# Moving weight sums of the mixing stage from VectorE to GpSimd in a fused transformer kernel

## The reference

```python
p = h @ w_in[l]                                   # q, k, v, gu, gv, conv input, gates
gl = a[..., :CONV_WIDTH] * jax.nn.sigmoid(a[..., CONV_WIDTH:])      # gated linear unit
y = depthwise_conv(gl, conv_w, taps=31) + conv_b
c_out = jax.nn.silu(layer_norm(y, norm_g, norm_b)) @ w_conv_o
gates = jax.nn.sigmoid(p[..., GATE_OFF:])                           # ga, gg, gc
return (ga * a_out + gg * g_out + gc * c_out) @ w_out
```

## Time and profile before

| | |
|---|---|
| median of three runs | 3959.73 us |
| the profiled execution, its span | 3959.4 us |
| TensorE busy | 3818.9 us, 96% |
| VectorE busy | 2353.0 us, 59% |
| ScalarE busy | 945.4 us, 24% |
| GpSimd busy | 290.0 us, 7% |
| mixing of block 0 | 555 to 1067 us |
| mixing of block 1 | 2205 to 2547 us |

### The profile page before, as it was taken

How to read it: one execution, slowest core, us unless ns; L and a number is a source line. 1 busy time by engine, 2 the same in 40 slices (tenths; PEclk the granted TensorE clock), 3 DMA queues, 4 the chain that set the end, 5 groups by cost and what they waited for, 6 DMA issues and landing times.

```text
span 3959.4 us, 34044 instructions
## 1 busy us (share of the span) xinstructions
PE 3818.9 (96%) x13274; PEld 2247.6 (57%) x13274; DVE 2353.0 (59%) x3855; ACT 945.4 (24%) x1917; POOL 290.0 (7%) x257
## 2 busy tenths in 40 slices
PE   7999899999999999999999999999999999889999
PEld 3454455555554555554445876647665458657665
DVE  5793548887405556556315699525667456835666
ACT  2102521111403111113125211321111334431111
POOL 1111000113021000000000012210000000000000
PEclk8999999999999999999999999999999999999999
DMA  7652001111212111111210112222222213011221
GB/s 262 216 198 90 6 22 58 48 55 52 96 61 59 64 64 53 54 64 54 72 68 6 64 65 85 85 101 80 85 90 88 75 34 88 9 43 64 91 96 69
DMA packets 126640, 300.51 MB, mean 76 GB/s; under 512 B 5394, under 2 KB 13634, under 8 KB 126480
## 3 DMA queue, kind: packets, MB, share of 16 engines
q1 hardware_dynamic: 108720, 239.73, 17.1%
q0 software_dynamic: 17760, 58.61, 4.5%
HBM read 296.14 MB, written 2.18 MB: 75 GB/s over the span
## 4 chain that ended last, share of the span: by engine, by line
PE 87%; DVE 8%; ACT 2%; DMA 1%; issue 1%; DVEq 0%; SPq 0%; ACTq 0%
PE psum L447 33%; PE psum L2495 15%; PE psum L2365 14%; PE psum L2419 12%; PE psum L2359 3%; PE psum L1127 2%; PE psum L2464 2%; PE psum L2447 1%; DVE sb_kvt L2813 1%; DVE sb_rc L2813 1%; PE psum L1233 1%; DMA sb_ra<-in_ada_w 1%; ACT sb_rb L2047 1%; DMA sb_ring<-in_ada_w 1%; PE psum L1253 1%
## 5 line engine op out<-in xcount | busy, mean ns | idle before, releaser
L447 PE MATMUL psum<-sb_ring,sb_rc 128*128 128x512 f32 x868 | 392.7, 594 | 7.5 <-DVE sb_rc L593 7.5
L2047 ACT ACTIVATE sb_rc<-psum 128x512 f32<-128x512 f32 (+3 forms) x295 | 147.1, 519 | 993.1 <-DVE sb_ra L609 294.7
L2903 DVE SCALAR_TENSOR_TENSOR sb_rc<-sb_rc,sb_vec 128x512 f32<-128x512 f32 (+1 forms) x450 | 384.2, 916 | 0.0
L2419 PE MATMUL psum<-sb_ring,sb_ht 128*128 128x512 f32 x832 | 364.5, 597 | 3.5 <-ACT sb_ht L2047 2.8
L447 PE MATMUL psum<-sb_ht,sb_ring 128*128 128x256 f32 (+1 forms) x1152 | 307.3, 417 | 0.0
L447 PEld LDWEIGHTS psum<-sb_ring,sb_rc 128*128 128x128 f32 x868 | 164.7, 190 | 216.6 <-issue 204.3
L2047 ACT ACTIVATE sb_rc<-sb_rc 128x512 f32<-128x512 f32 (+3 forms) x248 | 152.8, 680 | 526.2 <-DVE sb_rc L578 526.2
L2495 PE MATMUL psum<-sb_ht,sb_ring 128*128 128x384 f32 (+1 forms) x960 | 274.0, 433 | 4.0 <-DVE sb_rc L3137 4.0
L2365 PE MATMUL psum<-sb_rc,sb_ring 128*128 128x512 f32 (+1 forms) x768 | 276.6, 521 | 0.0
L2419 PEld LDWEIGHTS psum<-sb_ring,sb_ht 128*128 128x128 f32 x832 | 156.8, 191 | 205.7 <-issue 202.3
L447 PE MATMUL psum<-sb_rb,sb_rc 128*128 128x512 f32 x588 | 269.2, 594 | 0.0
(11 more groups left out here) (414 smaller groups left out, 5580.1 us busy)
## 6 DMA issues: line engine op xcount, KB each, us to landing
sb_ring<-in_w_in SPq DMA_DIRECT2D x37, 2048.0 KB, 7.9
sb_ring<-in_w_ff SPq DMA_DIRECT2D x32, 2048.0 KB, 8.0
sb_ring<-in_w_ffn SPq DMA_DIRECT2D x16, 2048.0 KB, 7.9
sb_rc<-in_ada_w POOLq DMA_DIRECT2D x26, 1024.0 KB, 5.8
sb_ra<-in_ada_w POOLq DMA_DIRECT2D x14, 1024.0 KB, 5.8
sb_ring<-in_w_gmlp_o SPq DMA_DIRECT2D x4, 2048.0 KB, 7.8
sb_ring<-in_w_attn_o SPq DMA_DIRECT2D x4, 2048.0 KB, 7.7
sb_ring<-in_w_conv_o SPq DMA_DIRECT2D x4, 2048.0 KB, 7.8
```

Source lines behind the costliest of these rows:

```text
L447: last = pe.matmul(bank(to, width), left[k], right[k], start=k == 0, stop=k == depth - 1)
L2047: return act.activation(out_, in_, f, **kw)
L2419: last = pe.matmul(bank(4 + g % 4, width), lhs[:, k, at:at + P], ring[:, slot, k, 0:width], start=k == 0, stop=k == KT - 1)
L2903: step = stt(out_, in_, vec[:, j, k:k + 1], out_, op0=ALU.mult, op1=ALU.add)
```

## The change

GpSimd gets a function `weight_sums` of its own, with the same four operations, and makes the sets of units 2 to 19 in both blocks. VectorE keeps those of units 0 and 1. For unit 2 GpSimd also waits until VectorE's two sets are counted, so that `s_mix_s` goes up in order. Sets 2 to 9 come one after another behind the pads. Sets 10 to 19 stand between the merges of branch outputs: in branches 0 and 1 one set before each of the merges 0, 2, 4 and 6, in branch 2 sets 18 and 19 before merge 0. In VectorE's order the calls are struck out and nothing is put in their place.

```diff
+            def weight_sums(l, u):
+
+                slot, loaded = mix_loaded(l, u)
+                pool.wait_ge(*loaded)
+                pool.wait_ge(*s_mix_ps.at(l, 6 * u - 7))
+                if u == 2:
+                    pool.wait_ge(*s_mix_s.at(l, 2))
+                a11, a12, a21, a22 = mix_weights(slot, u)
+                s_ = mix_sums(u)
+                tt = pool.tensor_tensor
+                ch.link(tt(s_[:, 0, :, :], a21, a22, ALU.add))
+                ch.note(tt(a21, a11, a21, ALU.subtract))
+                ch.link(tt(s_[:, 1, :, :], s_[:, 0, :, :], a11, ALU.subtract))
+                tt(s_[:, 2, :, :], a12, s_[:, 1, :, :], ALU.subtract).then_inc(s_mix_s.sem, 1)
...
+                for u in range(2, 10):
+                    weight_sums(l, u)
                 for b in range(3):
                     run = 3 * l + b
                     for j in range(KT):
+                        first = 10 + 4 * b + 2 * (j // 4)
+                        if b < 2 and j % 2 == 0:
+                            weight_sums(l, first + j % 4 // 2)
+                        if b == 2 and j == 0:
+                            weight_sums(l, 18)
+                            weight_sums(l, 19)
                         pool.wait_ge(*s_bo_sb.at(run, j + 1))
...
                     third_sum(l, u)
-                    if u < 8:
-                        weight_sums(l, u + 2)
                     if u >= 4 and (u < 9 or u % 2 == 0):
...
-                        weight_sums(l, u + 1)
                         convolve(f3)
-                        weight_sums(l, u + 2)
                         convolve(f3)
...
                     step(l, 16)
-                weight_sums(l, 18)
...
                 third_sum(l, 17)
-                weight_sums(l, 19)
```

## The result

Eight runs of the kernel with the change have the median 3969.3 us (3967.21 to 3972.81); eight of the kernel before beside them 3959.56 us (3956.65 to 3962.33). The ratio is 1.0024, with a 95% interval of 1.0014 to 1.0034: slower, by 9.7 us at the medians.

The account below looks back on a forecast made before the run. The prediction took TensorE's unbroken matmul chain as the bound, so freeing VectorE gains nothing; stalls of 3.6 + 1.8 + 1.4 + 2.9 = 9.7 us on 3959.4 gave 3969 us, range 3959 to 3986.

Parts of the forecast that it names:

- Nothing to win, and the chain: Both mixing stretches: an unbroken run of matmuls, VectorE holds nobody up, at most 1.4 us of idle TensorE to win.
- 1.02 us for each operation: VectorE's taps: delay per GpSimd operation beside them; a moved set costs a busy VectorE 4.08 us where it saved 2.66.
- Units 4 to 9: Both blocks: sets delay VectorE's third sums, TensorE waits for ScalarE's copies; 3.6 us in block 1, 1.8 in block 0.
- together 8.0: Unit 7's third sum, block 1: sets 6, 7 and 8 leave 3.9 us of lateness, set 9 adds 4.08.
- reserves of 4.4 and 6.1 us: Unit 7: slack between ScalarE's copy and the product needing it, 4.36 us in block 1, 6.1 in block 0.
- Unit 14 of block 1: Set 14 waits for the tap stream's end, merges 0 and 1 queue behind it; stall 1.4 us, ends 0 and 4.
- Before the norm: Before the convolution's norm, block 1: GpSimd's queue of sets 16, 17 and merges runs late; stall 2.9 us, ends 0 and 6.
- ScalarE waits for merge 7 before its first squares: Before block 1's norm: merge 7 ends at 2512.8, ScalarE's fourth copy of unit 16 at 2514.3, against a reserve of 1.1.
- sets 18 and 19 cost nothing: Before their units: ready 6 to 10 us ahead on a free GpSimd, no cost; 2 us if it were late.
- The base: Whole kernel: profiled span 3959.4 us, median of three runs 3959.73, with nothing but 0.3 around the span.
- The rival that the contention would be absorbed: Taps are filler, VectorE terms halve, GpSimd queue terms vanish: 2.7 us, 3962.1; chance 0.43.
- GpSimd would be the bound: At 1.8 us an operation, unit 7 and sets 10, 12, 14 run late: 32 us, 3991; chance 0.07 above 3986.

Follow-up runs that it names:

- e12: Kernel after with only sets 2 to 5 and 10 to 15 on GpSimd, VectorE waiting for its own last operation twice per long tap stream; 3960.7 us, ratio 1.0.
- e7: Kernel after, GpSimd's sets 6 to 9 waiting for the third sum of the unit two before them; 3965.6 us, single execution.
- e5a: Kernel after, first operation of sets 2 to 9 made twice on GpSimd, one more operation that reads SBUF; 3976.6 us, single execution.
- e1: Kernel after with only sets 2 to 9 of each block on GpSimd, 10 to 19 back on VectorE; 3967.1 us, ratio 1.002.
- e8: Kernel after, one convolution tap less in three places of each of units 4 to 8, five more behind units 10, 12 and 14; 3969.0 us, single execution.
- e9: Kernel after, VectorE waiting for its own last operation at two places of the long tap streams behind units 9, 11, 13 and 15; 3971.0 us, single execution.
- e6: Kernel after, set 17 put behind merge 7 of the second branch in GpSimd's queue; 3966.4 us, single execution.
- e11: Kernel after with only sets 2 to 5, 10 to 15, 18 and 19 on GpSimd, VectorE waiting for itself twice per long tap stream; 3961.0 us, ratio 1.0003.
- e2: Kernel after with only sets 10 to 19 of each block on GpSimd, 2 to 9 back on VectorE; 3964.7 us, ratio 1.0015.
- e5b: Kernel after with a 128x512 memset on GpSimd ahead of the first operation of sets 2 to 9; 3971.2 us, single execution.
- e1b: The kernel of e1 run again, only sets 2 to 9 of each block on GpSimd against the kernel after; 3963.3 us.

## Why the prediction was right, and where it was not

The forecast of 3969 us met the median of 3969.3, and the loss of 9.7 us is the sum of the terms. That is partly luck. Two terms were too high, one place had a second bound that the prediction left out, and what made up for the two high terms was not in the sum. The waits alone lost 0.43 + 7.2 = 7.6 us; 1.7 us of slower clock in the profiled execution and 0.3 us outside the span bring it near 9.7.

- **Nothing to win, and the chain.** Right. No run, e12 included, came out under the kernel before.
- **1.02 us for each operation.** Right: 1.01 for an operation that falls wholly beside taps, in unit 7 of the kernel after, in e7 and for block 0 in e5a; 0.97 for each of the eight subtractions, (12.66 - 4.90) / 8, with GpSimd's queue beside them without a gap. The price came from two merges of the old trace.
- **Units 4 to 9.** The mechanism is shown by e1, e5a, e7 and e8. The size was too high: 2.8 against 3.6 us, and 0.4 against 1.8. The failing step is the lateness of unit 7's third sum, "together 8.0": measured from the start of the mixing it was 7.0 us late in block 1 (2298.52 - 2205.16 against 2291.75 - 2205.43), and 6.4 in block 0 in place of 7.9. Set 9's 4.05 is right, the three sets before it left 3.0 and 2.4 us, not 3.9 and 3.8. Sets 7 and 8 cost VectorE 3.6 to 3.8 us each and not 4.08, as part of an operation fell beside a sum that reads PSUM and was not delayed (0.41 us at 2265.54). The reserves of 4.4 and 6.1 us held.
- **Unit 14 of block 1.** 1.45 against 1.4 us, shown by e9: the set waited until the stream was over, and its merges stood behind it. 7.65 us for an operation of 1.26, and 1.40 as soon as the stream had a break. By the rule of the Trainium skill (SBUF — State Buffer, "Who interferes with whom") the second waits for one instruction, so it would have got in after one tap; the measurement decides, and it waited for all that were left, nine behind the one that ran.
- **Before the norm.** The failing step is "ScalarE waits for merge 7 before its first squares": true, but not the only bound. e6 took it away and 2.12 of 2.30 us stayed. I had counted GpSimd's queue and left out what that queue does to VectorE's subtractions. The 2.9 us met the lateness without clock, 4.65 - 1.7 = 3.0, since both chains end together and since the 0.4 us at the convolution's mean, which the sum had not, came on top of 2.55. That sets 18 and 19 cost nothing failed as well in e11, where two operations of set 18 beside the subtractions go with 1.26 us of idle time; in the kernel after no such piece stands apart from the larger stall.
- **A term that was missing.** The clock: 1.7 us behind the longest wait, in the profiled execution after, and not in every execution.
- **The base.** I took 0.3 us around the span; it is 1.8 for the kernel before and 2.1 for the kernel after. By my estimate the profiled execution before took 3959.4 + 1.8 = 3961.2 us, above the median of 3959.56, and its time outside the mixing was 1.8 us longer than in the execution after. These two errors nearly cancelled.

The rival that the contention would be absorbed, 3962 us, needed a price under 0.85 us for an operation. That GpSimd would be the bound needed 1.8 us alone; its sets took 1.26 or 1.27 us an operation where VectorE was quiet, as the merges had.

## What to carry to other kernels

Before work goes from VectorE to GpSimd, look for a place in the old trace where GpSimd reads SBUF beside VectorE's work on SBUF, and take the delay per operation from it: here 1.01 us for VectorE against the 0.67 us that the operation had cost there, a loss even with VectorE's time alone in the account. It is the place of each operation that decides: look which of VectorE's results is next on the path, with what reserve, and look at every result behind it too: e7 took the stall away in one unit and had half of it back in the next, and e8 paid for units 7 and 8 with larger stalls later. Where two chains meet at one wait, work out both before removing one.

## What was not expected of the hardware

**Starving.** GpSimd's first operation that came 10 to 26 taps into a long stream of VectorE's ended 1.1 us after the stream's last tap: 7.65 us at 2437.18 and 17.40 us for one in block 0. A wait of VectorE for its own last tap brought these to 1.40 and 5.32 us, again with the end 1.1 us behind the break.

**The clock falls behind idle time, in some executions only.** Behind the same wait before the norm, 2.1 to 2.3 us, the granted clock fell to about 0.5 in the kernel after, e2 and e5b and not in e5a, e6, e7 and e9. It also fell behind 2.54 us in unit 8 of e5a and behind 2.87 and 2.24 us in e8. Each fall costs 1.4 to 1.7 us. The same happens where the kernel has always had a wait: behind 2.23 us of idle time at the start of the mixing of block 0 the first eight matmuls took 2.85 us in eight of the profiles and 4.12 to 4.41 us in the six others. The window there in e1b:

```profile
555.00:560.00 5.00, 5.00 (x12) 0.66 0.02 3
```

Behind the waits of 1.85 us and less in the mixing no profile shows a fall. So a stall has a price beyond its length that not every profile shows, and part of the spread of the times, 3955.2 to 3965.2 us for the kernel before in 21 runs of one chip, may be such falls; the traces show them, the share of the spread was not measured.
